# Norm factors moved behind the products in the second block, and a mirrored Fourier stage

## The chip, the cores and the metric

The kernel runs as one program on one core of a Trainium2 chip. The metric is the device time of one execution in microseconds (us); the median of several executions is compared. A profiled execution is recorded once for each kernel, and all rows below come from it.

## The reference

Two blocks follow each other on one sequence of 512 positions with 1024 channels, all in float32. The first block also carries 256 context positions and has a Fourier layer and a recurrent layer, each followed by a mixture of experts. The second has two layers with a mixer (gated MLP, state-space part, latent attention) and a squared-ReLU MLP. What matters here:

```python
def rmsnorm_2(x, g):
    var = jnp.mean(xf * xf, axis=-1, keepdims=True)
    return (xf * lax.rsqrt(var + EPS)).astype(x.dtype) * g

def fourier_mix(h, w_o, b_o):           # 4 groups of 256 channels, positions and channels transformed
    f = jnp.fft.fft2(hg, axes=(1, 3), norm='ortho').real
    return f.reshape(bsz, t, D_MODEL).astype(h.dtype) @ w_o + b_o

x = rmsnorm(x, final_g)                 # end of the first block
for l in range(DEPTH):                  # second block, DEPTH = 2
    h = rmsnorm_2(x, norm_mix_g[l])
    uv, z, xbc, dt_raw, c_q, c_kv, k_rope = split_cols(h @ w_in[l])
    ...                                 # latent attention: rmsnorm_2(c_q, ..) @ w_qb, rmsnorm_2(c_kv, ..) @ w_kvb
    x = x + mix @ w_out[l]
    x = x + squared_relu_mlp(rmsnorm_2(x, norm_mlp_g[l]), mlp_w1[l], mlp_w2[l])
return rmsnorm_2(x, final_norm_g)
```

Since the MLP squares its ReLU, a positive factor on its input comes out as its square on its output.

## The kernel before

Channels lie on the 128 partitions in eight tiles (`KT`), positions along the free axis: `X` holds the residual stream, `H` the normalised input of a stage, `scr` is a scratch area that stages carve up by offset (`S(off, ...)`). Weights stream through a ring of eight slots of 1 MB in the fixed order of `weight_plan`; SyncE issues the load of a slot as soon as the slot's last reader is done. PSUM has eight banks that `bank()` hands out in turn; the next user waits for `free.<name>`. Each engine has one counting semaphore; `did` counts and names steps, `later`/`at` wait for a named step. Each engine runs the list of stages in its own order; `phase()` at the end of a stage makes an engine wait until the other engines have ended that stage too, except, for TensorE, VectorE and ScalarE, in `mla` and `mix`.

A float32 matmul appears in the profile as two records; the MLP's are of another kind, one record each: its operands are split into a rounded high part and the rest (`HHI`, `WHI` on ScalarE, the rests on VectorE), and three products are made of them (L2571 to L2573, L2586 to L2588).

A norm (`fg`, `n20`, `n30`, `n21`, `n31`, `end`) is squares on ScalarE (L371 or L387), their sum over tiles on VectorE (L379), a product with ones on TensorE (L418), the reciprocal root on ScalarE (L393), and eight multiplies of `X` with gain and factor into `H` on VectorE (L434). Squares and sums of most tiles are made as the residual tiles come (`residual_scalar`, `residual_vector`, L538/L540). After `moe1` come `fg`, a copy of H to X (L2783), and `n20`. Then `mla` makes six latent products (L1961 three of c_q, L1970 two of c_kv, L1976 rotary key with dt), the sums of their squares (L1984), the products q (L1992, six), k (L2002) and v (L2007), and scores (L2021). VectorE turns the rotary parts (L2110 to L2116 for k, L2129 to L2134 for q) and applies the latent norms (L2124). `wout` makes the output products (L2313), `mlp` follows.

The Fourier stage makes for each of 6 position tiles and 4 channel groups a product with cosine and sine of 256 (512 columns, L561), evicted to `Z`; then for each of 8 channel tiles and both segments the products with the position tables (L574), evicted to `H` (L601); then the output products (L520). Between them stand blocks of the adaLN parameters (`ada_tensor`, L454 and L463), 1 MB of weights each.

Of the kernel before, what the change touches and what calls it, by code (L numbers as in the profile page):

```python
# [25 lines left out]
P = 128  # L26
# [109 lines left out]
def build(nc, a, out, table):  # L136
# [3 lines left out]
    with ctx:  # L140
# [143 lines left out]
        DFT_C = S(12288, 2, 512)  # L284
# [77 lines left out]
        NEXT = {"moe0": "n1", "post": "m1", "moe1": "fg", "wout0": "n30", "mlp0": "n21", "wout1": "n31", "mlp1": "end"}  # L362
        EARLY = list(NEXT.values()) if STOP is None else list(NEXT.values())[:-1]

        def residual_scalar(act, tag, segs, norm, tiles=range(KT)):

            w = sum(s[1] for s in segs)
            for m in tiles if norm in EARLY else ():
                if later(act, f"{tag}.x{m}"):
                    act.wait_ge(*at(f"{tag}.x{m}"))  # L370
                did(A_, act.activation(H[:, m, 0:w], X[:, m, 0:w], ACT.Square).then_inc(scalar_done, 1), f"{norm}.sq{m}")  # L371

        def norm_sum(dve, norm, k, w):
# [3 lines left out]
            if later(dve, f"{norm}.sq0"):  # L377
                dve.wait_ge(*at(f"{norm}.sq0"))
            did(V, dve.tensor_tensor(H[:, 0, 0:w], H[:, 0, 0:w], H[:, k, 0:w], ALU.add).then_inc(vector_done, 1))  # L379
# [32 lines left out]

        def norm_tensor(pe, tag, segs):
# [24 lines left out]
        small_rs = S(SCRW - TA, TA)  # L438

# [88 lines left out]
        def residual_vector(dve, tag, segs, gate=None, norm=None, tiles=range(KT)):  # L528
# [4 lines left out]
            for m in tiles:  # L533
                for i, (s0, sn) in enumerate(segs):
                    t = tile(dve, f"{tag}.{m}.{s0}")
                    x = X[:, m, s0:s0 + sn]
                    if gate is None:
# [4 lines left out]
                marks[f"{tag}.x{m}"] = (V, count[V])  # L542
                if norm in EARLY and m >= 2:
                    norm_sum(dve, norm, m - 1, w)
            if norm in EARLY and KT - 1 in tiles:
# [3 lines left out]
        Z = S(0, 6, 4, 512)  # L549
        fb = small[:, 0:16].rearrange("p (k c) -> p k c", c=2)  # L550

        def fnet_tensor(pe):
            if later(pe, "dft"):
                pe.wait_ge(*at("dft"))
            for tt in range(6):
                for g in range(4):
                    b = bank(pe, f"f1.{tt}.{g}")
                    for k in range(2):
                        if later(pe, f"n0.h{2 * g + k}"):
                            pe.wait_ge(*at(f"n0.h{2 * g + k}"))  # L560
                        ins = pe.matmul(b, H[:, 2 * g + k, tt * P:tt * P + P], DFT_C[:, k, :], start=k == 0, stop=k == 1)  # L561
                    did(T_, ins.then_inc(tensor_done, 1), f"f1.{tt}.{g}")
                    if (4 * tt + g) % 3 == 2:
                        ada_tensor(pe, ADA_F1[0] + (4 * tt + g) // 3)
            for s0, sn, tts in ((TX, TC, (4, 5)), (0, TX, (0, 1, 2, 3))):
                for d in range(KT):
                    b = bank(pe, f"f2.{d}.{s0}")
                    for cs in range(2):
                        for n, tt in enumerate(tts):
                            if later(pe, f"free.f1.{tt}.{d // 2}"):  # L570
                                pe.wait_ge(*at(f"free.f1.{tt}.{d // 2}"))
                            rhs = DFT_T[:, n, cs * TX:cs * TX + TX] if s0 == 0 else DFT_TC[:, n, cs * TC:cs * TC + TC]
                            o = cs * 256 + (d % 2) * P
                            ins = pe.matmul(b[:, 0:sn], Z[:, tt, d // 2, o:o + P], rhs,  # L574
                                            start=cs == 0 and n == 0, stop=cs == 1 and n == len(tts) - 1)
                    did(T_, ins.then_inc(tensor_done, 1), f"f2.{d}.{s0}")
                    if d % 2:
                        ada_tensor(pe, ADA_F2[0] + (0 if s0 else 4) + d // 2)
            linear_tensor(pe, "fo", "fwo", lambda k, s0, sn: H[:, k, s0:s0 + sn], SEGS, lambda k: f"free.f2.{k}.0",
                          between=lambda n: ada_tensor(pe, ADA_FO[0] + n))  # L580

        def fnet_scalar(act):
            for tt in range(6):
# [2424 lines left out]
```

## Time and profile before

| | |
|---|---|
| median of 3 runs | 4090.1 us (4081.94 to 4090.91) |
| profiled execution, its own time | 4094.43 us |
| its span, first to last instruction | 4092.6 us |
| TensorE busy | 3697.3 us, 90% of the span |
| VectorE busy | 1310.9 us, 32% |
| ScalarE busy | 1017.0 us, 25% |
| mean granted TensorE clock | 0.959 |

A busy time says how long an engine had work, not whether that work held anything up; for that the chain of work that ended last is read, and the timeline of the stretch. The granted clock is a share of 2.4 GHz and is either 1.00 or 0.50, so a mean between them is a stretch that holds both. Spacing from one start to the next is used for the length of a product, because the recorded ends of pipelined matmuls overlap.

### The profile page before, as it was taken

What the parts mean: (1) busy time and instruction counts of PE and PEld (TensorE: products, weight loads), DVE (VectorE), ACT (ScalarE), POOL (GpSimd) and SP (SyncE); (2) the same over time, 40 slices, a digit from 0 to 9 for tenths busy, and PEclk for the clock granted to TensorE, in tenths of its full rate; (3) what the DMA queues carried; (4) which work ended last, traced back from release to release, by engine and by line L of the source; (5) the groups of instructions that cost most, each with busy time, mean ns of one, the idle gap of its engine ahead of it and who ended that gap; (6) DMA issues with size and microseconds to landing.
All of it is one profiled execution on the core that took longest, in us unless ns stands there. A gap on an engine that the chain in (4) does not pass through costs nothing.

```text
span 4092.6 us, 63317 instructions
## 1 busy us (share of the span) xinstructions
PE 3697.3 (90%) x28370; PEld 2279.9 (56%) x28370; DVE 1310.9 (32%) x2368; ACT 1017.0 (25%) x1974; POOL 260.6 (6%) x232
## 2 busy tenths in 40 slices
PE   6998999999799989998867887879989998998998
PEld 3556443433357678888352332235548884656886
DVE  2123000000443167776330000025433333444342
ACT  3012011111143155454110000114322221423231
POOL 0000000000000144433000000000000000000000
PEclk9987999999889999999979999989999999999999
DMA  8345889898035244332429999901222322112320
GB/s 292 103 139 173 306 307 362 313 351 294 0 141 183 65 112 92 68 83 77 141 103 381 375 375 387 351 23 48 71 62 93 93 83 77 48 52 78 98 97 21
DMA packets 530928, 666.74 MB, mean 163 GB/s; under 512 B 156553, under 2 KB 299145, under 8 KB 530657
## 3 DMA queue, kind: packets, MB, share of 16 engines
q1 hardware_dynamic: 520544, 633.40, 45.8%
q10 hardware_dynamic: 6912, 18.88, 1.2%
q0 software_dynamic: 3200, 10.42, 0.7%
q8 instruction: 223, 3.65, 0.4%
q14 instruction: 49, 0.39, 0.0%
HBM read 631.18 MB, written 31.46 MB: 162 GB/s over the span
## 4 chain that ended last, share of the span: by engine, by line
PE 76%; DVE 8%; DMA 5%; SPq 4%; ACT 3%; POOL 3%; issue 1%; DVEq 0%; ACTq 0%; POOLq 0%
PE ps L657 12%; PE ps L662 4%; DMA ring<-in_moe_wu 4%; SPq L2710 4%; PE ps L520 3%; PE ps L850 3%; PE ps L2571 3%; PE ps L2572 3%; PE ps L2573 3%; PE ps L2587 3%; PE ps L2588 3%; PE ps L2586 3%; PE ps L823 3%; PE ps L2207 3%; PE ps L2313 3%; POOL ring L1403 3%
## 5 line engine op out<-in xcount | busy, mean ns | idle before, releaser
L657 PE MATMUL ps<-ring,H 128*64 128x512 f32 x2048 | 494.2, 601 | 52.1 <-DMA ring<-in_moe_wu 39.2
L657 PEld LDWEIGHTS ps<-ring,H 128*64 128x64 f32 x2048 | 147.3, 137 | 343.0 <-issue 252.4
L759 DVE TENSOR_TENSOR scr<-ps,scr 128x512 f32<-128x512 f32 x32 | 22.1, 692 | 965.5 <-PE ps L662 516.9
L657 PE MATMUL ps<-ring,scr 128*64 128x512 f32 x1024 | 248.3, 599 | 40.3 <-DMA ring<-in_moe_wd 38.8
L2571 PE MATMUL ps<-scr_rounded,ring_rounded 128*128 128x512 f32 x512 | 204.8, 400 | 23.0 <-ACT scr_rounded L2609 23.0
L2640 DVE TENSOR_TENSOR ring_rounded<-ring,scr_rounded 128x2048 fp32r<-128x2048 f32 x64 | 146.7, 2293 | 227.6 <-ACT scr_rounded L2606 227.5
L2572 PE MATMUL ps<-H_rounded,scr_rounded 128*128 128x512 f32 x512 | 204.6, 400 | 0.0
L2573 PE MATMUL ps<-scr_rounded 128*128 128x512 f32 x512 | 204.3, 399 | 0.0
L2588 PE MATMUL ps<-scr_rounded 128*128 128x512 f32 x512 | 202.5, 395 | 0.0
L2586 PE MATMUL ps<-scr_rounded,ring_rounded 128*128 128x512 f32 x512 | 201.8, 394 | 0.0
L2606 ACT ACTIVATE scr_rounded<-ring 128x2048 fp32r<-128x2048 f32 x64 | 122.1, 1907 | 257.7 <-PE ps L2588 246.4
L657 PEld LDWEIGHTS ps<-ring,scr 128*64 128x64 f32 x1024 | 72.9, 136 | 189.2 <-issue 125.1
L850 PE MATMUL ps<-scr 128*128 128x512 f32 (+1 forms) x320 | 125.9, 556 | 4.2 <-ACT scr L733 2.9
L823 PE MATMUL ps<-scr 128*128 128x256 f32 x512 | 121.4, 390 | 4.0 <-DVE scr L930 4.0
L2571 PEld LDWEIGHTS ps<-scr_rounded,ring_rounded 128*128 128x128 f32 x512 | 97.5, 190 | 48.8 <-DVE H_rounded L2645 24.6
L662 PE MATMUL ps<-ring,H 128*32 128x256 f32 x2048 | 123.8, 382 | 0.0
L727 ACT ACTIVATE scr<-ps 64x512 f32<-64x512 f32 x64 | 37.9, 592 | 313.0 <-PE ps L662 161.5
L2207 PE MATMUL ps<-H,ring 128*128 128x512 f32 x256 | 111.3, 594 | 0.0
L2572 PEld LDWEIGHTS ps<-H_rounded,scr_rounded 128*128 128x128 f32 x512 | 97.6, 191 | 23.6
L2313 PE MATMUL ps<-scr,ring 128*128 128x512 f32 x256 | 110.7, 593 | 0.0
L2573 PEld LDWEIGHTS ps<-scr_rounded 128*128 128x128 f32 x512 | 97.3, 190 | 23.6
L2586 PEld LDWEIGHTS ps<-scr_rounded,ring_rounded 128*128 128x128 f32 x512 | 96.1, 188 | 23.9
(403 smaller groups left out, 6123.9 us busy)
## 6 DMA issues: line engine op xcount, KB each, us to landing
ring<-in_moe_wg SPq DMA_DIRECT2D x128, 1024.0 KB, 9.5
ring<-in_moe_wu SPq DMA_DIRECT2D x128, 1024.0 KB, 8.6
ring<-in_moe_wd SPq DMA_DIRECT2D x128, 1024.0 KB, 10.3
ring<-in_mlp_w SPq DMA_DIRECT2D x64, 1024.0 KB, 5.5
ring<-in_ada_w SPq DMA_DIRECT2D x48, 1024.0 KB, 7.4
ring<-in_w_in SPq DMA_DIRECT2D x14, 1024.0 KB, 5.2
ring<-in_w_out SPq DMA_DIRECT2D x8, 1024.0 KB, 5.1
st_kka<-scr ACTq DMA_DIRECT2D x16, 384.0 KB, 3.5
```

What stands on the lines that cost most here:

```text
L657: ins = pe.matmul(bx[64 * n:64 * n + 64, :], stat_x(k), w[:, k % 4, :], start=k == 0, stop=k == KT - 1)
L662: ins = pe.matmul(bc[32 * n:32 * n + 32, 0:256], stat_c(k), w[:, k % 4, o:o + 256], start=k == 0, stop=k == KT - 1)
L823: ins = pe.matmul(b[:, 0:256], HT[:, tt, k * P:k * P + P], GM[:, tt, :], start=tt == 0, stop=tt == 3)
L850: ins = pe.matmul(b[:, 0:sn], ys[:, j, m * P:m * P + P], sm[:, j, :], start=j == 0, stop=j == nj - 1)
L2207: ins = pe.matmul(b, w[:, k, (m % 2) * P:(m % 2) * P + P], H[:, k, 0:TX], start=k == 0, stop=k == KT - 1)
L2313: ins = pe.matmul(banks[m], w[:, k, (m % 2) * P:(m % 2) * P + P], MIX[:, k, :], start=k == 5, stop=k == 4)
L2571: pe.matmul(b, low[:, k, o], hh, start=k == 0, stop=False)
L2572: pe.matmul(b, high[:, k, o], hl, start=False, stop=False)
L2573: ins = pe.matmul(b, high[:, k, o], hh, start=False, stop=k == KT - 1)
L2586: pe.matmul(banks[m], low[:, k, o], hh, start=f == 0, stop=False)
L2588: ins = pe.matmul(banks[m], high[:, k, o], hh, start=False, stop=f == 15)
L2710: did(f"slot{i % NSLOT}", sp.dma_start(dst, src.rearrange("(k p) c -> p k c", p=min(P, rows))).then_inc(sems[f"slot{i % NSLOT}"], 16), "w. ...
```

## The change

Second block: the stages between `moe1` and the end lose `fg`, and no engine waits for the others at the end of `moe1`, `n2*`, `n3*`, `wout*`, `mlp*` (GpSimd still does). `residual_vector` writes the unnormalised `H = gain * X` per tile, and ScalarE squares X elsewhere (`SQUARES`), for `n20` also gain times X. `fg` and `n20` become one pass: with q0 and q1 the two mean squares, the factor for `n20` is the reciprocal root of q1 + eps*(q0 + eps), and X itself is scaled later. The latent products take the unnormalised H; the sum product runs behind the first of them; the latent norms need no factor (only eps is scaled by the mean square), the rotary key and dt are multiplied by it, then all of H. For `n3*`, high and low parts of H are made tile by tile during `wout`, the sum product runs behind the first MLP product, and `1/(mean square + eps)` multiplies each second MLP product before it is added. The last norm keeps its form; its result leaves in four stores.

Fourier: the channel transform of a group makes 129 cosine and 127 sine columns (256 in place of 512). Cosine column 128 of the four groups is gathered in `ZH` and transformed once per segment. The second transform makes four blocks per segment; the mirrored channels are the same block read backwards in position, and `fnet_wo`'s rows are permuted to fit.

```diff
-            if e != "G" and name[:3] in ("mla", "mix"):
+            if e != "G" and (name[:3] in ("mla", "mix", "wou", "mlp") or name[:2] in ("n2", "n3") or name == "moe1"):
...
+            if norm in SQUARES:
+                for m in tiles:
+                    if later(act, f"{tag}.x{m}"):
+                        act.wait_ge(*at(f"{tag}.x{m}"))
+                    for n, sq in enumerate(SQUARES[norm]):
+                        scale = col("final_g", m) if n else 1.0
+                        did(A_, act.activation(sq[:, m, :], X[:, m, 0:TX], ACT.Square, scale=scale).then_inc(scalar_done, 1))
...
+        def scaled_vector(dve, norm, m):
+            dve.wait_ge(*own(dve, V))
+            l = int(norm[2])
+            if norm == "n20":
+                ins = dve.tensor_scalar(H[:, m, 0:TX], X[:, m, 0:TX], col("final_g", m), col("nmix", m), ALU.mult, ALU.mult)
+            else:
+                ins = dve.tensor_scalar(H[:, m, 0:TX], X[:, m, 0:TX], col("nmix" if norm == "n21" else "nmlp", 8 * l + m), None, ALU.mult)
+            did(V, ins.then_inc(vector_done, 1), f"{norm}.u{m}")
+
+        def low_vector(dve, norm, m):
+            t0 = HIGH[norm]
+            if later(dve, f"{t0}hh{m}"):
+                dve.wait_ge(*at(f"{t0}hh{m}"))
+            did(V, dve.tensor_tensor(H_r[:, m, 0:TX], H[:, m, 0:TX], HHI[:, m, :].bitcast(F32), ALU.subtract).then_inc(vector_done, 1), f"{t0}hl{m}")
...
+                    if scale is not None:
+                        dve.wait_ge(*own(dve, V))
+                        did(V, dve.tensor_tensor(scale[1], t, scale[0], ALU.mult).then_inc(vector_done, 1), f"free.{tag}.{m}.{s0}")
+                        dve.wait_ge(*own(dve, V))
+                        did(V, dve.tensor_tensor(x, scale[1], x, ALU.add).then_inc(vector_done, 1))
+                        continue
...
+                if norm in SQUARES:
+                    scaled_vector(dve, norm, m)
+                    if norm in HIGH and m == 6:
+                        low_weights(dve, int(norm[2]), 0)
+                    if norm in HIGH and m:
+                        low_vector(dve, norm, m - 1)
...
             for tt in range(6):
+                for gg in range(2):
+                    b = bank(pe, f"f1.{tt}.{gg}")
+                    for g in (2 * gg, 2 * gg + 1):
+                        o = 256 * (g % 2)
+                        for k in range(2):
+                            ins = pe.matmul(b[:, o:o + 256], H[:, 2 * g + k, tt * P:tt * P + P], DFT_C[:, k, :], start=k == 0, stop=k == 1)
+                    did(T_, ins.then_inc(tensor_done, 1), f"f1.{tt}.{gg}")
+                    if (2 * tt + gg) % 3 < 2:
+                        ada_tensor(pe, ADA_F1[0] + (2 * tt + gg) // 3 * 2 + (2 * tt + gg) % 3)
...
+                for g in (0, 2):
+                    t = tile(dve, f"f2.{g}.{s0}")
+                    did(V, dve.tensor_copy(H[:, 2 * g + 1, s0 + 1:s0 + sn], t[:, sn - 1:0:-1]).then_inc(vector_done, 1))
+                    did(V, dve.tensor_copy(H[:, 2 * g + 1, s0:s0 + 1], t[:, 0:1]).then_inc(vector_done, 1))
+                    did(V, dve.tensor_copy(H[:, 2 * g, s0:s0 + sn], t[:, 0:sn]).then_inc(vector_done, 1), f"free.f2.{g}.{s0}")
...
+            latent("cq", 0, f"{t0}cq.0", 0)
+            sums_tensor(pe, hk)
+            latent("cq", 1, f"{t0}cq.0", P)
+            latent("cq", 2, f"{t0}cq.1", 0)
+            latent("ckv", 0, f"{t0}ckv", 0)
+            latent_norm("cq", 3)
+            latent("ckv", 1, f"{t0}ckv", P)
+            latent("kr", "", f"{t0}kr", 0)
+            latent_norm("ckv", 2)
...
+            for k in range(KT):
+                did(V, dve.tensor_tensor(H[:, k, 0:TX], H[:, k, 0:TX], RMS, ALU.mult).then_inc(vector_done, 1), f"{hk}.h{k}")
+            for k in range(KT) if l == 0 else ():
+                did(V, dve.scalar_tensor_tensor(X[:, k, 0:TX], X[:, k, 0:TX], col("final_g", k), RMS1, ALU.mult, ALU.mult).then_inc(vector_done, 1))
             for h in range(6):
...
+                        if f == 0:
+                            sums_tensor(pe, f"n3{l}")
...
+            low_weights(dve, l, 1)
+            mean_vector(dve, f"n3{l}", MSQ)
+            did(V, dve.reciprocal(MSQ, MSQ).then_inc(vector_done, 1))
...
+            for k in range(0, KT, 2):
+                if later(sp, f"end.h{k + 1}"):
+                    sp.wait_ge(*at(f"end.h{k + 1}"))
+                did("out", sp.dma_start(out.rearrange("(k p) t -> p k t", p=P)[:, k:k + 2], H[:, k:k + 2, 0:TX]).then_inc(output_out, 16), by=16)
```

## Rows read from the trace of the kernel before

**Rows 1.** The page, part 4: shares of the chain that ended last.

```profile
PE 76%; DVE 8%; DMA 5%; SPq 4%; ACT 3%; POOL 3%; issue 1%; DVEq 0%; ACTq 0%; POOLq 0%
```

**Rows 2.** TensorE's timeline, Fourier stage: start, us, line, operation, shape, count, idle before.

```profile
61.49 5.42 PE L561 MATMUL ps<-scr,H 128*128 128x512 f32 x12
66.84 1.07 PE L454 MATMUL ps<-ring,csil 128*32 128x256 f32 x16
114.18 3.70 PE L574 MATMUL ps<-scr 128*128 128x256 f32 x16
117.81 1.07 PE L454 MATMUL ps<-ring,csil 128*32 128x256 f32 x16
119.28 3.70 PE L574 MATMUL ps<-scr 128*128 128x256 f32 x16
129.47 13.98 PE L574 MATMUL ps<-scr 128*128 128x512 f32 x32
144.85 13.98 PE L574 MATMUL ps<-scr 128*128 128x512 f32 x32
```

**Rows 3.** TensorE's timeline from moe1 to layer 0's first score.

```profile
2689.76 7.03 PE L850 MATMUL ps<-scr 128*128 128x512 f32 x16
2725.58 22.67 PE L1961 MATMUL ps<-H,ring 128*128 128x512 f32 x48 [6.26 <-DVE H L434]
...
2803.48 0.39 PE L2021 MATMUL ps<-scr 96*128 96x128 f32 x2
```

**Rows 4.** Timeline of VectorE there: the multiplies of the second norm.

```profile
2720.14 5.39 DVE L434 SCALAR_TENSOR_TENSOR H<-X,vec,scr 128x512 f32<-128x512 f32 x8 [3.00 <-ACT scr L393]
```

**Rows 5.** Timeline of TensorE: mlp0's last product and layer 1's first score.

```profile
3395.14 0.40 PE L2588 MATMUL ps<-scr_rounded 128*128 128x512 f32 x1
...
3483.30 0.39 PE L2021 MATMUL ps<-scr 96*128 96x128 f32 x2
```

**Rows 6.** Timelines: layer 0's last residual add (VectorE), first MLP product (TensorE).

```profile
3018.98 0.69 DVE L538 TENSOR_TENSOR X<-ps,X 128x512 f32<-128x512 f32 x1 [5.58 <-PE ps L2313]
...
3033.82 0.77 PE L2571 MATMUL ps<-scr_rounded,ring_rounded 128*128 128x512 f32 x1 [11.51 <-ACT scr_rounded L2609]
```

**Rows 7.** The page, part 5: busy us, mean ns, idle before, releaser.

```profile
L2571 PE MATMUL ps<-scr_rounded,ring_rounded 128*128 128x512 f32 x512 | 204.8, 400 | 23.0 <-ACT scr_rounded L2609 23.0
L2640 DVE TENSOR_TENSOR ring_rounded<-ring,scr_rounded 128x2048 fp32r<-128x2048 f32 x64 | 146.7, 2293 | 227.6 <-ACT scr_rounded L2606 227.5
```

**Rows 8.** The output: SyncE's timeline, and the DMA issues (KB, us to landing).

```profile
4084.99 0.38 SPq L2717 DMA_DIRECT2D outT<-H  x1
...
outT<-H SPq DMA_DIRECT2D x1, 2048.0 KB, 7.2
```

**Rows 9.** Windows: us; busy by engine; granted clock; DMA share; GB/s.

```profile
54.00:58.00 4.00, 4.00 (x7) 1.73 (x8) 0.69 (x1) 0.00 (x0) 0.00 (x0) 0.67 1.10 348
78.00:82.00 4.00, 4.00 (x27) 1.75 (x26) 0.69 (x1) 0.98 (x2) 0.00 (x0) 1.00 0.32 110
300.00:312.00 12.00, 12.00 (x92) 6.26 (x84) 11.96 (x16) 3.19 (x12) 0.00 (x0) 0.50 0.88 281
3038.00:3040.00 2.00, 2.00 (x6) 1.54 (x6) 2.00 (x1) 0.00 (x0) 0.00 (x0) 0.53 0.00 0
```

**Rows 10.** VectorE's timeline in layer 0's latent attention, before the scores.

```profile
2768.99 0.68 DVE L2110 COPY scr<-ps 6x512 f32<-6x512 f32 x1 [43.46 <-PE ps L1976]
2773.72 3.60 DVE L2124 SCALAR_TENSOR_TENSOR scr<-scr,vec 128x512 f32<-128x512 f32 x5
2780.38 0.69 DVE L2129 TENSOR_TENSOR scr<-ps,scr 32x512 f32<-32x512 f32 x1 [3.06 <-PE ps L1992]
```

**Rows 11.** The chain that ended last: start, us, what, records.

```profile
2761.99 6.88 PE ps L1976 x16
2775.95 17.39 PE ps L1992 x36
...
4069.77 0.23 PE ps L2586
```

More of the change, by code:

```diff
@@ L411, in norm_scalar, with sums_tensor, mean_vector @@
                 shift_scalar(act, tag, segs)
+        def scaled_vector(dve, norm, m):
[11 more added lines that the diff above has]
+            did(V, dve.tensor_tensor(H_r[:, m, 0:TX], H[:, m, 0:TX], HHI[:, m, :].bitcast(F32), ALU.subtract).then_inc(vector_done, 1), f"{t0}hl{m}")
+        def sums_tensor(pe, norm):
+            if later(pe, f"{norm}.sum"):
+                pe.wait_ge(*at(f"{norm}.sum"))
+            for n, sq in enumerate(SQUARES[norm]):
+                b = bank(pe, f"{norm}.ss{n}")
+                did(T_, pe.matmul(b, ones[:, :], sq[:, 0, :], start=True, stop=True).then_inc(tensor_done, 1), f"{norm}.ss{n}")
+        def mean_vector(dve, norm, to, tmp=None):
+            t = tile(dve, f"{norm}.ss0")
+            if norm == "n20":
+                did(V, dve.tensor_scalar(tmp, t, 1.0 / D, EPS, ALU.mult, ALU.add).then_inc(vector_done, 1), f"free.{norm}.ss0")
+                t = tile(dve, f"{norm}.ss1")
+                did(V, dve.tensor_scalar(to, t, 1.0 / D, None, ALU.mult).then_inc(vector_done, 1), f"free.{norm}.ss1")
+                dve.wait_ge(*own(dve, V))
+                did(V, dve.scalar_tensor_tensor(to, tmp, EPS, to, ALU.mult, ALU.add).then_inc(vector_done, 1))
+            else:
+                did(V, dve.tensor_scalar(to, t, 1.0 / D, EPS, ALU.mult, ALU.add).then_inc(vector_done, 1), f"free.{norm}.ss0")
+            marks[f"{norm}.mean"] = (V, count[V])
+            dve.wait_ge(*own(dve, V))
         def norm_tensor(pe, tag, segs):
@@ L555, in fnet_tensor @@
             for tt in range(6):
-                for g in range(4):
[L557 to L564, printed above, removed]
@@ new lines, in fnet_tensor, with table_of @@
+            for s0, sn, tts in ((TX, TC, (4, 5)), (0, TX, (0, 1, 2, 3))):
+                def table_of(n, cs):
+                    return DFT_T[:, n, cs * TX:cs * TX + TX] if s0 == 0 else DFT_TC[:, n, cs * TC:cs * TC + TC]
+                for tt in tts:
+                    for gg in range(2):
+                        if later(pe, f"free.f1.{tt}.{gg}"):
+                            pe.wait_ge(*at(f"free.f1.{tt}.{gg}"))
+                b = bank(pe, f"fh.{s0}")
+                for n, tt in enumerate(tts):
+                    ins = pe.matmul(b[:, 0:sn], ZH[:, tt, :], table_of(n, 0), start=n == 0, stop=n == len(tts) - 1)
+                did(T_, ins.then_inc(tensor_done, 1), f"fh.{s0}")
+                for g in range(4):
+                    b = bank(pe, f"f2.{g}.{s0}")
@@ L568, in fnet_tensor @@
                     for cs in range(2):
                         for n, tt in enumerate(tts):
[L570 to L574, printed above, removed]
+                            ins = pe.matmul(b[:, 0:sn], Z[:, tt, g, cs * P:cs * P + P], table_of(n, cs),
@@ L1918, in build @@
         MIX = S(0, KT, TX)
+        MEAN, RMS, MEAN1, RMS1 = (MIX[:, n, :] for n in range(4))
         CQ = S(4096, 3, TX)
@@ L2850, in _ @@
                     norm_scalar(act, st, XSEG, True)
[L2851 removed]
+                elif st == "end":
                     norm_scalar(act, st, XSEG, False)
```

265 lines of the change are left out of this document (157 added, 108 removed).

## The prediction

> **What bounds the kernel now.** I read the page first. TensorE holds 76% of the chain that ended last, VectorE 8%, ScalarE 3% [rows 1]. So time can be won in two ways: fewer TensorE columns where TensorE never waits, or closing the holes in which it waits for a chain of short instructions on the other two. Then I read the timeline of TensorE at the two places that the diff touches.
>
> The Fourier stage has no holes. In the first transform twelve records of 512 columns and one adaLN block alternate; in the second the period is 5.10 us (114.18 to 119.28) for the 256 context positions and 15.38 us for the 512 positions, each with one adaLN block of 1.47 us (117.81 to 119.28) [rows 2].
>
> In the second block there are holes. The last product of moe1 ends at 2696.8 (2689.76 + 7.03), mla0's first starts at 2725.58: 28.8 us, two norms one behind the other [rows 3], each a sum product, a root on ScalarE and eight multiplies of 5.39 us on VectorE [rows 4]. A shorter one follows mlp0, whose last product ends about 3395.4 [rows 5]. Layer 0's output products end just before VectorE's add at 3018.98, at about 3018.9; the MLP starts at 3033.82, 14.95 us later [rows 6]. Both layers have this hole: the group of the first MLP products shows 23.0 us of idle in all behind ScalarE's high parts, 11.5 per layer [rows 7]. At the end one store goes out at 4084.99 and lands 7.2 us later [rows 8]. After each hole TensorE also runs at 1.2 GHz for a while: after 3033.82 the granted clock is 0.50 until nearly 3040 (0.53 over the last 2 us) [rows 9].
>
> **Fourier stage, first transform.** 12 groups of 4 products of 256 columns take the place of 24 groups of 2 products of 512. It stays at 96 records. A 512-column record takes 5.35/12 = 0.446 us (61.49 to 66.84), one of 256 columns 3.63/16 = 0.227 [rows 2]: 42.8 becomes 21.8, 21.0 less. Two things are given back. The last group now has no adaLN block behind it, so the second transform waits for its eviction, two copies and a one-column copy: between nothing and three operations of 0.7 [rows 10]; I take 1.3, as the copies are 256 wide. And the warm-up: the stage starts at 1.2 GHz, and the clock rises after some 3 us of dense products (mean 0.67 over 54 to 58) [rows 9]. Now 3.4 us of products are followed by a light adaLN block, and such blocks alone left the clock at 0.50 for the 12 us from 300 to 312 [rows 9]. Bounds: nothing if it rises in the first group, 7.5 us if it takes the two groups that stand back to back (18 us at half speed cost 9, of which 1.5 is paid today). I take 2. Gain 21.0 - 1.3 - 2 = 17.7 us.
>
> Could the adaLN weights be late? They come at 348 GB/s with the queues full (share 1.10); over 78 to 82 the share is 0.32, so by then the eight-deep ring was full and waited for TensorE [rows 9]. ada.15, the last that the stage needs, was therefore in before 78; the shorter stage wants it at about 83. No wait.
>
> **Second transform.** One half-spectrum block and four blocks per segment in place of eight. Context: 4 x 5.10 = 20.4 becomes 4 x (8 x 0.227 + 1.47) + 4 x 0.227 = 14.1. The 512 positions, a record (15.38 - 1.47)/32 = 0.435: 61.5 becomes 4 x (16 x 0.435 + 1.47) + 8 x 0.435 = 37.2 [rows 2]. 30.6 us less. The mirrored evictions (reverse copy, copy, one column, one row) are in no row; four operations of 0.7 make 2.8 us, under 8.4 us per group, and the last group has an adaLN block and six products, 1.5 + 5.2 us, ahead of its first reader. Cost nothing; 2 us if reverse reads took three times as long. Fourier together 48.3 us.
>
> **moe1 to the first score of layer 0.** The unnormalised h is written while moe1's last products run (eight products, 6.9 us per tile; VectorE needs 2.6), so mla0's first product starts at once and only its eighth matmul waits for the last tile. From there: six latent products of 6.88 = 41.3, five latent sums 4.3, q 36 x 0.430 = 15.5 [rows 11], k and v 2803.48 - 2775.95 - 17.39 = 10.1 [rows 3, 11]: 71.2 us, and 0.86 for each norm's sum product (two records). Layer 0 has two: 72.9. Today it is 2803.48 - 2696.8 = 106.7 [rows 3].
> What is late next is VectorE. It sits at the latent sum until 47.2 us; k's rope, broadcast and the latent norms today take 2768.99 to 2777.3, 8.3 us, of which three of five norms, 2.2, come earlier now [rows 10]; two new operations of 0.7 come on top, then H times the factor and X times gain and factor, 5.4 each by the nearest row [rows 4]. The q ropes start near 47.2 + 6.1 + 1.4 + 10.8 = 65.5, each three operations, 2.1 us [rows 10]. k's third product needs the bank of q0, and so on to the first score, which needs that of q5: 65.5 + 5 x 2.1 + 1.4 = 77.4. So 4.5 us of delay; bounds 0 (small waits overlap) and 8. Gain 106.7 - 77.4 = 29.3. It holds two spells of half clock: 22.67 us for 48 records that take 20.6, and 17.39 for 36 that take 15.5 [rows 3, 11].
>
> **mlp0 to the first score of layer 1.** Today 3483.30 - 3395.4 = 87.9 [rows 5]. Afterwards 71.2 + 0.9 = 72.1; X gets no second norm, the ropes start near 60 and q5's bank is free at 72. Gain 15.8, bounds 13 and 16.
>
> **Output products to MLP, twice.** Per tile VectorE adds, scales, subtracts the high part and sums, four operations of 0.5 to 0.7, 2.6 us against tiles of 2.6 and then 6.9 us; the weight split, 2.3 us [rows 7], goes behind tile 6 under 6.9 us. The last low tile comes 3.4 us behind the last product; the first MLP product wants it after 21 matmuls of 0.234 [rows 11], 4.9 us. No hole: 14.95 us, and 3.0 for 6.1 us at half clock [rows 6, 9], less 0.86 for the sum product: 17.1, twice 34.2. Bounds 15 and 18 each.
> Behind the products stand a reciprocal (no row; even 5 us, once per layer) and one more multiply per residual tile. They lie in weight slots of 48 x 0.234 = 11.2 us, of which VectorE has 2.3 + 4 x 0.7 = 5.1 in use [rows 7, 10, 11]. Without that cover 16 tiles per layer would cost 22 us in all.
>
> **End.** One more multiply, +0.7. The output leaves in four stores, the first 4.0 us before the last multiply ends. If bytes bound it, the end is 4081 + 7.2 = 4088.2 in place of 4092.2 [rows 8]; if nothing of the store shrinks but its start, 2 us less is won. 3.3, bounds 1 and 4.
>
> **Sum.** 48.3 + 29.3 + 15.8 + 34.2 + 3.3 = 130.9. The profiled execution took 4094.4 (span 4092.6 and 1.8 around it); 3963.5. The median shown is 4.3 below the profiled run: 3959.2; for small waits that I left out I say 3961.
>
> **Rivals.** (a) The first transform stays at 1.2 GHz: 96 x 0.454 + 8 x 2.6 (12 us hold 92 records, 20 per block [rows 9]) = 64 us in place of 37, time 3988. For it: adaLN blocks never raised the clock. Against it: two groups stand back to back in every third place, 6.8 us, longer than the 3 to 6 us after which it rose at 57 and 3040 [rows 9]. Chance 0.05. The Trainium skill (TensorE: Matmul & The Clock Gate, "What's actually happening") says that the throttled state is the default and that activity releases it; by that rule the thinned first transform could be kept slow, the 27 us above, where I take 2; the row at 300 agrees with it, the row at 54 does not decide [rows 9].
> (b) VectorE is late behind the norms by more than summed: 4 us more in each latent stage, 3 us in front of each MLP, reverse reads 2: 3977. For it: its work in these stretches doubles. Chance 0.08.
> (c) Slower than before: VectorE sets the MLP's pace. All 64 slots would have to grow by 131/64 = 2.0 us, so VectorE would need 13.3 us per slot where it uses 5.1, price 64 us per microsecond beyond. Time over 4100. The split's row has more idle (227.6) than work (146.7) [rows 7]. Chance 0.01.
> (d) The holes close but the clock does not stay up, 9 us back, and the stores win nothing: 3973. Chance 0.08.
> Forecast, 3945 to 3970: 0.78.
>
> **Numbers.** 0.2%, about what a measurement can tell, is 8 us; all cases but (c) lie far beyond. The range takes the lower bounds and the runs' own spread (9 us) below, (b) and (d) and the other bounds above, and leaves out (a) and (c): 3942 to 3985. Faster 0.98, same 0.01, slower 0.01.
>
> **What would show it.** The second transform starts near 91, the stage's output products near 142; mla0's first product stands directly behind moe1's last; no TensorE hole over 1 us before either MLP and clock 1.00 there; the k to score stretch is stretched by 4.5 us in layer 0 and hardly in layer 1. The prediction is wrong if TensorE waits for VectorE over 8 us before a first score, or if adaLN blocks near 75 still run at half clock.

## The result, and the profile after

The changed kernel took 3956.6 us (median of 4 runs, 3954.8 to 3959.3) beside 4086.5 us for the kernel before on the same chip (4 runs, 4081.9 to 4090.9): a ratio of 0.9683, with a 95% interval of 0.9666 to 0.970. The forecast was 3961.0, the range 3942 to 3985. The profiled execution took 3957.2 us; its span is 3955.4 where the kernel before had 4092.6, so 137.2 us went.

First the page of the changed kernel: part 4 (shares of the chain that ended last) and two rows of part 5 (busy us, mean ns, idle before).

```profile
PE 76%; DVE 9%; DMA 5%; SPq 4%; ACT 3%; POOL 2%; issue 1%; DVEq 0%; ACTq 0%; POOLq 0%
...
L2725 DVE TENSOR_TENSOR ring_rounded<-ring,scr_rounded 128x2048 fp32r<-128x2048 f32 x64 | 146.7, 2292 | 218.9 <-ACT scr_rounded L2718 218.6
L2743 PE MATMUL ps<-scr_rounded,ring_rounded 128*128 128x512 f32 x512 | 203.6, 398 | 0.0
```

The shares hardly moved, since the whole shrank by only 3%. The second of the two groups is the one with 23.0 us of idle in [rows 7]: now it has none.

TensorE's timeline of the Fourier stage in the changed kernel (start, us, line, shape, count, idle before and who ended it), and windows with the granted clock behind the POOL column:

```profile
54.26 3.59 PE L645 MATMUL ps<-scr,H 128*128 128x256 f32 x8 [10.51 <-ACT H L427]
57.78 1.07 PE L519 MATMUL ps<-ring,csil 128*32 128x256 f32 x16
58.78 1.99 PE L645 MATMUL ps<-scr,H 128*128 128x256 f32 x8
...
87.58 1.97 PE L645 MATMUL ps<-scr,H 128*128 128x256 f32 x8
90.46 1.10 PE L658 MATMUL ps<-scr 128*128 128x256 f32 x4 [0.91 <-ACT scr L680]
...
116.75 7.11 PE L664 MATMUL ps<-scr 128*128 128x512 f32 x16
...
142.28 4.11 PE L585 MATMUL ps<-H,ring 128*128 128x512 f32 x9
```

```profile
54.00:58.00 4.00, 3.74 (x12) 2.66 (x16) 0.82 (x3) 0.16 (x1) 0.00 (x0) 0.55 1.10 348
58.00:62.00 4.00, 4.00 (x43) 2.41 (x35) 0.78 (x3) 1.26 (x5) 0.00 (x0) 1.00 1.10 349
```

The first group of eight products runs at 1.2 GHz (3.59 us), the second at 2.4 (1.99 us). The adaLN block between them does not bring the clock down (1.00 from 58 to 62). Where the two transforms meet, TensorE waits 0.91 us for the last eviction.

TensorE from moe1's last product to the first scores of layer 0, then VectorE in the same stretch, then TensorE in front of layer 1's first score, all of the changed kernel:

```profile
2643.75 2.74 PE L972 MATMUL ps<-scr 128*128 128x512 f32 x6
2646.32 7.03 PE L2084 MATMUL ps<-H,ring 128*128 128x512 f32 x16
...
2719.08 1.56 PE L2125 MATMUL ps<-ring,scr 128*128 128x384 f32 x4 [0.60 <-DVE scr L2283]
2721.24 1.56 PE L2125 MATMUL ps<-ring,scr 128*128 128x384 f32 x4 [0.60 <-DVE scr L2283]
2723.49 0.46 PE L2139 MATMUL ps<-scr 96*128 96x128 f32 x2 [0.70 <-DVE scr L2283]
```

```profile
2700.88 4.91 DVE L2275 TENSOR_TENSOR H<-H,scr 128x512 f32<-128x512 f32 x8
2705.71 5.39 DVE L2277 SCALAR_TENSOR_TENSOR X<-X,vec,scr 128x512 f32<-128x512 f32 x8
2711.12 0.69 DVE L2280 TENSOR_TENSOR scr<-ps,scr 32x512 f32<-32x512 f32 x1
```

```profile
3363.20 5.32 PE L2125 MATMUL ps<-ring,scr 128*128 128x384 f32 x16
3368.36 0.39 PE L2139 MATMUL ps<-scr 96*128 96x128 f32 x2
```

The 28.8 us between the first two lines of [rows 3] are gone: mla0's first product stands directly behind moe1's last. What is late next is VectorE: its query rotations (L2280 to L2285) begin at 2711.12, behind the eight multiplies of H and the eight of X, and TensorE waits for them in front of each group of four value products and at the score: 0.18, three times 0.60 and 0.70 us of idle. In layer 1, where X gets no factor, the score waits for nothing.

At the MLP (TensorE in layer 0), and at the end (SyncE and the DMA issues of the end: KB, us to landing):

```profile
2924.57 12.61 PE L2466 MATMUL ps<-scr,ring 128*128 128x512 f32 x29
2936.61 0.79 PE L2743 MATMUL ps<-scr_rounded,ring_rounded 128*128 128x512 f32 x1
```

```profile
3946.33 5.39 DVE L495 SCALAR_TENSOR_TENSOR H<-X,vec,scr 128x512 f32<-128x512 f32 x8 [2.16 <-ACT scr L417]
3947.77 4.35 SPq L2873 DMA_DIRECT2D outT<-H  x4
```

```profile
outT<-H SPq DMA_DIRECT2D x4, 512.0 KB, 3.3
```

The first MLP product follows the output products without a wait, where [rows 6] had 11.51 us of idle. The granted clock from 2936 to 2944 is 1.00.

### The profile page after: what moved, and what is told of

Its sections match the earlier page's. It is cut to its first block, busy times and chain, and to the rows that moved or that the text cites. A ratio compares the mean times of both kernels' runs of the same rounds, so it can differ in the third digit from the quotient of the medians.

```text
span 3955.4 us, 63217 instructions
## 1 busy us (share of the span) xinstructions
PE 3628.6 (92%) x28286; PEld 2254.3 (57%) x28286; DVE 1341.8 (34%) x2430; ACT 1018.0 (26%) x1996; POOL 260.2 (7%) x232
## 4 chain that ended last, share of the span: by engine, by line
PE 76%; DVE 9%; DMA 5%; SPq 4%; ACT 3%; POOL 2%; issue 1%; DVEq 0%; ACTq 0%; POOLq 0%
PE ps L779 12%; PE ps L784 5%; DMA ring<-in_moe_wu 4%; SPq L2865 4%; PE ps L585 3%; PE ps L972 3%; PE ps L2745 3%; PE ps L2761 3%; PE ps L2762 3%; PE ps L2744 3%; PE ps L2760 3%; PE ps L2743 3%; PE ps L945 3%; PE ps L2360 3%; PE ps L2466 3%; PE ps L2084 2%
## 5 line engine op out<-in xcount | busy, mean ns | idle before, releaser
L972 PE MATMUL ps<-scr 128*128 128x512 f32 (+1 forms) x320 | 125.9, 556 | 4.2 <-ACT scr L855 2.9
L611 DVE SCALAR_TENSOR_TENSOR X<-ps,ada,X 128x512 f32<-128x512 f32 (+1 forms) x48 | 31.8, 662 | 241.8 <-PE ps L972 119.9
L862 ACT ACTIVATE scr<-ps 128x512 f32<-128x512 f32 x32 | 19.1, 597 | 358.7 <-PE ps L784 196.2
L2743 PEld LDWEIGHTS ps<-scr_rounded,ring_rounded 128*128 128x128 f32 x512 | 96.1, 188 | 24.3 <-issue 1.0
## 6 DMA issues: line engine op xcount, KB each, us to landing
ring<-in_ada_w SPq DMA_DIRECT2D x48, 1024.0 KB, 10.3
```

The costliest lines, as they stand in the source:

```text
L972: ins = pe.matmul(b[:, 0:sn], ys[:, j, m * P:m * P + P], sm[:, j, :], start=j == 0, stop=j == nj - 1)
L2743: pe.matmul(b, low[:, k, o], hh, start=k == 0, stop=False)
```

## The experiments

All twelve profiled executions beside the two kernels, cut at starts of TensorE products (the last cut at the span's end). Times are us of the traces; the names of the columns say what a stretch ends with (for a score, the product with the identity that starts 0.2 to 0.3 us behind it): the Fourier stage's first product, the first output product of that stage, the first router product of moe0, the last product of moe0, that of moe1, the first score of layer 0, the first product of mlp0, the first score of layer 1, the end.

```
                      start Fourier router  moe0    moe1  score0  mlp0  score1   end
before                 53.8  137.2  131.8  758.9  1614.5  107.5  230.1  449.7  609.1
changed                54.3   88.0  125.9  759.5  1618.2   77.9  212.8  432.0  586.8
e1 Fourier alone       53.8   88.0  125.9  759.5  1614.8  107.5  230.1  449.7  609.7
e2 block 2 alone       52.4  138.5  125.7  759.2  1615.0   77.9  212.9  431.9  587.1
e3 engines meet        52.4   87.8  125.9  759.4  1615.2   83.9  217.3  439.5  595.8
e6 scale twice         53.3   88.7  131.2  758.8  1614.5   77.9  212.8  432.0  588.7
e7 changed again       53.1   88.6  131.2  758.8  1611.3   77.9  212.9  431.9  587.2
e4 one store           53.5   88.1  126.0  759.5  1618.0   77.9  212.8  431.9  593.5
e5 X's norm later      54.8   88.3  126.0  756.5  1611.8   73.6  212.8  432.0  586.2
e8 interleaved         53.3   88.7  117.3  758.9  1614.6   78.0  212.8  432.0  587.0
e9 both                54.9   88.6  117.3  758.9  1613.6   73.6  214.6  431.9  586.9
e11 interleaved again  54.2   89.1  117.4  759.2  1617.2   77.9  214.6  431.9  587.7
e10 before, interl.    52.8  138.6  119.0  759.2  1614.6  107.5  230.1  449.7  609.8
e12 before, no meet.   54.8  137.7  125.3  759.0  1611.3  101.7  228.4  443.4  609.0
```

Read the table by columns. Where an edit does not touch a stretch, most stretches repeat within a microsecond. The exceptions are the router column, which has two values for one kernel (below), the moe1 column (1611.3 to 1618.2, in no relation to any edit; what varies there, no run shows), moe0 in e5 (756.5), the Fourier column (up to 1.4 us apart) and the column that ends with mlp0 (212.8 or 214.6). That last difference lies in the mixer, where the granted clock stands at 0.50 for 6.8 us (2822.4 to 2829.2 in the changed kernel) or for 10.3 (2899.9 to 2910.2 in the kernel before).

### e1 and e2: each part alone

e1 is the kernel before with the new Fourier stage:

```diff
-        DFT_C = S(12288, 2, 512)
+        DFT_C = S(12288, 2, 256)
...
-    c["dftC"] = np.concatenate([cs, sn], 1)
+    c["dftC"] = np.concatenate([cs[:, 0:129], sn[:, 1:128]], 1)
...
+    n["fnet_wo"] = n["fnet_wo"][:, np.concatenate([mirrored[:, 0:128], mirrored[:, 128:256]], 1).reshape(-1), :]
...
```

with the new `fnet_tensor`, `fnet_scalar` and copies of `fnet_vector`; e2 is the changed kernel with those lines and functions put back.

> The kernel before with the mirrored Fourier stage and nothing else of the change. Theory of the prediction: the two parts add, so 4086.5 less 17.7 for the first transform and 30.6 for the second, 48.3 in all, gives 4038 us (ratio 0.988), with the first transform at 36 to 38 us of the trace, the second at 51 to 53 and the output projection unchanged. Rival: the first transform runs at half the clock here and wins nothing, 4056 us. Rival: the shorter stage meets weights that come no earlier and waits for them behind the stage, 4050 us or more. The second block must take what it took in the kernel before.

> The changed kernel with the old Fourier stage, its table and the old order of the output weights. Theory of the prediction: 29.3 + 15.8 + 34.2 + 3.3 = 82.6 us less than 4086.5, so 4004 us (ratio 0.980). In the trace of the changed kernel 5.9 us of the gain were in the norm in front of the first mixture of experts, where the instructions are the same and only TensorE's granted clock differs: if that is a matter of chance, this run's stage takes either 36 or 42 us, whatever the Fourier stage is. Rival: that difference comes from the Fourier stage, so this run has 42 us there and the run with the Fourier stage alone has 36.

e1 took 4039.0 us and e2 4005.5 (4038 and 4004 were expected), beside 4089.4 for the kernel before in that set: ratios 0.9868 (0.9852 to 0.9885) and 0.9791 (0.9776 to 0.9806). Their product is 0.966, the whole change 0.968 (0.9666 to 0.970): within these intervals the parts add. In the table e1 changes the Fourier column by 49.2 us and no column of the second block, and e2 the reverse. The router column is 125.9 and 125.7 in both, so these runs give its 5.9 us to neither part; e7, below, shows them come and go in one program.

### e3 and e12: the meetings of the engines

e3 is the changed kernel with the old rule, e12 the kernel before with most of the new one:

```diff
 # e3
-            if e != "G" and (name[:3] in ("mla", "mix", "wou", "mlp") or name[:2] in ("n2", "n3") or name == "moe1"):
+            if e != "G" and name[:3] in ("mla", "mix"):
 # e12
-            if e != "G" and name[:3] in ("mla", "mix"):
+            if e != "G" and (name[:3] in ("mla", "mix", "wou") or name[:2] == "n2" or name == "moe1"):
```

> The changed kernel, but all engines meet again at the end of each stage of the second block, apart from the attention and mixer stages, as in the kernel before. The factors stay behind the products. Theory A (the gain comes from the products that need no finished norm; the meetings are a smaller part): TensorE then waits at four places (behind the last expert product, behind both output projections and behind the first MLP) for one eviction of 0.7 us, one scaling of 0.7 us, one square and one sum, 3.5 to 4.5 us each, and 1 us each for the clock: 16 to 22 us more than the changed kernel, 3973 to 3979 us. Theory B (the meetings were what cost the time): 60 us or more come back, 4017 us or more. Theory C (meetings are free where the next products wait for the same data): within 4 us of the changed kernel.

> The kernel before without the meeting of the engines behind the last experts, behind both output projections and behind the norm in front of each attention stage (the two norms in front of the MLPs, the final norm of the first block and the MLPs still end in one). Theory A (a meeting costs only where the next products have their data): the products still wait for the finished norm; what is won is that the first of them follows the first norm tile and not the eighth, 1.5 to 2 us at each of two places: 4082 to 4084 us, within 0.15 per cent of the kernel before. Theory B (the meetings cost by themselves what they cost in the changed kernel): at least 12 of its 23 us, 4074 us or less.

e3 took 3980.9 us (ratio 0.9733, 0.9716 to 0.9749), 23 to 24 more than the changed kernel: theory A, a little over the upper end of its 16 to 22. TensorE in e3 behind moe1 and in front of mlp0:

```profile
2645.31 8.83 PE L2084 MATMUL ps<-H,ring 128*128 128x512 f32 x16 [4.02 <-DVE scr L398]
...
2941.85 0.50 PE L2743 MATMUL ps<-scr_rounded,ring_rounded 128*128 128x512 f32 x1 [3.90 <-DVE scr L398]
```

The waits are 4.02 and 3.90 us (3.4 behind mlp0), as expected. The clock's part was too small in the expectation: the 16 latent products take 8.83 us, where they take 7.03 in the changed kernel. With its clock a meeting costs 5.6 to 6.3 us: 6.0 behind moe1, 6.3 behind mlp0, and 4.5 in front of each MLP with 1.2 more in the MLP's first 48 products, which the next column holds. In the last column 3.3 of the 9.0 us come from light mixer products of layer 1 that happened to run at 1.2 GHz.

e12 took 4072.9 us (ratio 0.9971, 0.996 to 0.9983), 13.4 less than the kernel before. By the number that is theory B (at least 12 us), not A's 2 to 4; by the mechanism most of it is what A names, the earlier start, which brings more than A gave it. The table has 13.8 us in three columns, 5.8, 1.7 and 6.3. VectorE's multiplies of the second norm and TensorE's first products in e12:

```profile
2711.99 5.39 DVE L434 SCALAR_TENSOR_TENSOR H<-X,vec,scr 128x512 f32<-128x512 f32 x8 [3.00 <-ACT scr L393]
2712.88 23.21 PE L1961 MATMUL ps<-H,ring 128*128 128x512 f32 x48 [1.71 <-DVE H L434]
```

Here the products start 0.9 us behind the first multiply; in the kernel before it was 5.44 ([rows 3], [rows 4]). I had reckoned with products at 2.4 GHz, which would have caught up with the multiplies and then gone at their pace, so that only the last tile counted. But TensorE comes out of a long wait at 1.2 GHz. The 48 products take 23.21 us in e12 and 22.67 in the kernel before: at that clock they are no faster than the multiplies, so of a start 4.5 us earlier 4.0 are kept, and the low clock lies beside VectorE's work. The other 1.7 of the first column's 5.8 are the query products, which here take 15.69 us and not the 17.39 of [rows 11]: the wait that they stand behind is the same 2.80 us in both, but the clock did not fall. In the third column the start is again 4.5 us earlier, of which 4.4 are kept; 0.6 are the norm's sum product and 1.3 the first products of mlp0, both less at 1.2 GHz, as is the middle column's 1.7, the mixer. So 8.4 of the 13.8 us are the earlier starts. The other 5.3 are shorter spells of 1.2 GHz; whether they follow from the edit or fell that way by chance, no run shows. So of the second block's 83 us (the sum of its terms) some 13, 8 of them traced to the earlier starts, could be had without moving a factor, about 59 without touching the meetings (83 less the 24 of e3), and the last 11 only with both.

### e6: is VectorE's room in the MLP real?

```diff
                     if scale is not None:
                         dve.wait_ge(*own(dve, V))
+                        did(V, dve.tensor_tensor(scale[1], t, scale[0], ALU.mult).then_inc(vector_done, 1))
+                        dve.wait_ge(*own(dve, V))
                         did(V, dve.tensor_tensor(scale[1], t, scale[0], ALU.mult).then_inc(vector_done, 1), f"free.{tag}.{m}.{s0}")
```

> The changed kernel with the multiplication of an MLP product by the reciprocal mean square done twice for each of the 16 tiles of each MLP: 32 more VectorE instructions of 0.69 us, 22 us of VectorE. Theory of the prediction: VectorE has room under the products in all but the last group of four tiles of each MLP, where up to 4 x 0.69 = 2.8 us lie open, so 1.4 to 5.5 us more than the changed kernel, 3958 to 3962 us. Rival (VectorE sets the pace of the MLP): all 22 us come back, 3979 us or more.

e6 took 3953.7 us (ratio 0.9667, 0.9652 to 0.9681): no loss that can be measured, of 22 us of added work. The score1 column does not move (432.0), the last one grows by 1.5 to 1.9 us, which is all that shows of the 1.4 to 5.5 expected. The prediction's cover holds, and rival (c) is out.

### e4: the four stores

```diff
-            for k in range(0, KT, 2):
-                if later(sp, f"end.h{k + 1}"):
-                    sp.wait_ge(*at(f"end.h{k + 1}"))
-                did("out", sp.dma_start(out.rearrange("(k p) t -> p k t", p=P)[:, k:k + 2], H[:, k:k + 2, 0:TX]).then_inc(output_out, 16), by=16)
+            if later(sp, f"end.h{KT - 1}"):
+                sp.wait_ge(*at(f"end.h{KT - 1}"))
+            did("out", sp.dma_start(out.rearrange("(k p) t -> p k t", p=P), H[:, :, 0:TX]).then_inc(output_out, 16), by=16)
```

> The changed kernel once more, as the measure for the three others of this set: 3956.6 us if nothing changes. The norm in front of the first mixture of experts (first square to first router product) takes 36 or 42 us of the trace: 36 again speaks for a difference that belongs to the kernel, 42 for chance.

> The changed kernel with the output stored by one transfer behind the last tile instead of four. Prediction: the single 2048 KB store took 7.2 us to land, a quarter of it 3.3 us, so 3.3 to 3.9 us more than the changed kernel, 3960 us. Rival (the stores win nothing, the end was shorter for another reason): no difference.

e7, the changed kernel again, took 3957.7 us and e4 3964.2, 6.4 more, where 3.3 to 3.9 were expected. VectorE's last multiplies and SyncE's store in e4, and the landing:

```profile
3948.07 5.39 DVE L495 SCALAR_TENSOR_TENSOR H<-X,vec,scr 128x512 f32<-128x512 f32 x8 [3.11 <-ACT scr L417]
3953.49 0.38 SPq L2872 DMA_DIRECT2D outT<-H  x1
```

```profile
outT<-H SPq DMA_DIRECT2D x1, 2048.0 KB, 7.3
```

From the last multiply's end to the span's end it is 3961.2 - 3953.46 = 7.7 us in e4, and 3955.4 - 3951.72 = 3.7 in the changed kernel: the stores are worth 4.0 us. The rest of the 6.7 us by which the last column of this execution grows is the clock's and not the store's: about 1.0 at the norm's sum product (2.08 us in place of 1.13), and 1.6 in the mixer of layer 1. Where the other executions lost the 2.4 us beyond the store's 4.0, no trace shows.

### e5: what is late next

```diff
-            for k in range(KT) if l == 0 else ():
-                did(V, dve.scalar_tensor_tensor(X[:, k, 0:TX], X[:, k, 0:TX], col("final_g", k), RMS1, ALU.mult, ALU.mult).then_inc(vector_done, 1))
             for h in range(6):
                 t = tile(dve, f"{t0}q{h}")
...
             did(V, dve.tensor_tensor_scan(DT4, RS6, DT0, 0.0, ALU.mult, ALU.add).then_inc(vector_done, 1), f"{t0}ac")
+            for k in range(KT) if l == 0 else ():
+                did(V, dve.scalar_tensor_tensor(X[:, k, 0:TX], X[:, k, 0:TX], col("final_g", k), RMS1, ALU.mult, ALU.mult).then_inc(vector_done, 1))
```

> The changed kernel, but the eight VectorE instructions of 0.67 us that put the final norm of the first block into the residual (5.3 us) stand no longer in front of the query rotations but in the mixer, in front of the convolution. Theory of the prediction: VectorE arrives last at the first scores of layer 0, so TensorE's 4.3 us of waits there go, and the mixer has VectorE idle for 13 us at the new place: 4 to 5 us less, 3952 us. Rival: the first score waits for the key or value evictions of ScalarE as well, so only 1 us is won. Rival: the mixer's convolution is then late, nothing is won.

TensorE in e5 in front of the first score:

```profile
2705.64 5.33 PE L2125 MATMUL ps<-ring,scr 128*128 128x384 f32 x16
2710.80 0.39 PE L2139 MATMUL ps<-scr 96*128 96x128 f32 x2
```

All 16 value products run in one piece and nothing is waited for. The score0 column goes from 77.9 to 73.6, by the 4.3 us expected, and the mixer's column stays at 212.8. In the times it shows less: 3956.4 us beside 3957.7, with single runs from 3943.8 to 3963.2. The 3943.8 is the execution of the trace, which was also 3.0 us shorter in moe0 and 6.4 in moe1 than the changed kernel's, where the edit has no part. The two intervals (0.9672 to 0.9699 and 0.967 to 0.9697) do not tell 4 us from none.

### e8, e10, e11 and e9: the clock in front of moe0

The instructions there are the same in both kernels, yet the changed one was 5.9 us faster. Windows of the changed kernel, then of e7, the same program once more (granted clock behind the POOL column):

```profile
238.00:250.00 12.00, 11.60 (x68) 6.55 (x68) 2.66 (x3) 3.97 (x17) 0.00 (x0) 0.52 0.98 299
250.00:258.00 8.00, 8.00 (x94) 4.34 (x96) 6.75 (x6) 4.11 (x14) 0.00 (x0) 0.87 0.75 241
```

```profile
238.00:250.00 12.00, 12.00 (x76) 6.35 (x80) 2.09 (x3) 4.33 (x15) 0.00 (x0) 0.53 1.02 313
250.00:258.00 8.00, 8.00 (x60) 4.36 (x56) 7.91 (x8) 2.11 (x8) 0.00 (x0) 0.50 0.77 249
```

One program, two courses: in both executions the clock falls at 238, but in the one it is back by 252, in the other it stays down over all blocks of the condition's product. The router column is 126 in one and 131 in the other. Of the ten executions without the edit below, seven had 125.3 to 126.0 and three 131.2 to 131.8. The Trainium skill (TensorE: Matmul & The Clock Gate, "What's actually happening") says that the point at which the clock rises differs from run to run of one kernel; the two pairs of lines agree. The difference that the Trainium skill gives there is half a microsecond; here the clock is back at 252 in one execution and at 297 in the other.

What makes it fall is in TensorE's timeline of the changed kernel: 3.68 us of idle behind ScalarE, which takes eight squares in one go before it evicts a block.

```profile
233.65 1.07 PE L519 MATMUL ps<-ring,csil 128*32 128x256 f32 x16
238.40 0.98 PE L528 MATMUL ps<-vec,scr 128*128 128x2 f32 x4 [3.68 <-ACT scr L544]
239.31 1.93 PE L519 MATMUL ps<-ring,csil 128*32 128x256 f32 x16
```

e8 puts an eviction behind every second square (e11 is e8 again, e10 the same edit in the kernel before, e9 both e5 and e8):

```diff
-                    squares_scalar(act, st, SEGS)
-                    for b in range(ADA_M0[0], half):
+                    for k in range(KT):
+                        did(A_, act.activation(H[:, k, 0:TA], X[:, k, 0:TA], ACT.Square).then_inc(scalar_done, 1), f"{st}.sq{k}")
+                        if k % 2:
+                            ada_scalar(act, ADA_M0[0] + k // 2)
+                    for b in range(ADA_M0[0] + 4, half):
                         ada_scalar(act, b)
```

> The changed kernel, but in the norm in front of the first mixture of experts ScalarE takes two squares, then the eviction of one block of the condition's product, and so on, where it took all eight squares first. In the trace TensorE stood for 3.68 us behind those squares, and its granted clock fell from 1.0 to about 0.5 behind it. Theory: without the stand TensorE keeps the clock, the sum product comes at 243 us of the trace in place of 247.6 and the stage ends 4 to 5 us earlier, 3952 us; if the clock fell for longer in the kernel before, the same edit would win 10 us there. Rival: the clock falls for the small products themselves, not for the stand, and only 1 to 2 us are won.

> The kernel with the interleaved squares once more, as the measure for the one before it in this set: 3946 us, with the stretch to the router at 117.3 us again, since TensorE does not stand there long enough for the chance of two outcomes that the changed kernel has (125.9 or 131.2).

> The kernel before with the interleaved squares only. Its stretch from the output projection's first product to the router took 131.8 us in its profiled execution. Theory (the stand behind the squares lowers the clock, and how long it stays low is chance): 117 us here too, so 8.6 to 14.5 us less than the kernel before, 4072 to 4078 us. Rival (the Fourier stage's change decides how long the clock is low): the edit wins 14 us in every execution.

> The changed kernel with both edits: the residual's final norm moved into the mixer, and the squares of the norm in front of the first mixture of experts taken in turn with the evictions of the condition's blocks. In the traces the first took 4.3 us off the stretch from the last expert product to the first score (77.9 to 73.6), the second brought the stretch from the output projection's first product to the router to 117.3 us from 125.9 or 131.2. The stretches are far apart, so they add: 3946.2 - 4.3 = 3942 us. Rival, from the times of the first edit alone (3956.4 beside 3957.7): it is given back where the trace did not look, and this kernel stays at 3945 to 3947 us.

e8 took 3946.2 us and e11 3946.5: 10 to 11.5 less than the changed kernel, about twice what was expected. The window of e8:

```profile
238.00:250.00 12.00, 11.12 (x128) 6.58 (x127) 9.44 (x9) 7.36 (x24) 0.00 (x0) 1.00 1.12 337
```

The clock stays at 1.00 and the router column is 117.3 and 117.4. The expectation took a sum product 4.6 us earlier; it came 6.8 us earlier (240.85 in place of 247.67), and the blocks behind it, which the expectation forgot, also run at 2.4 GHz now.

e10 took 4081.3 us beside 4086.2 (ratio 0.999, 0.9981 to 0.9999): 5 us, less than the 8.6 to 14.5 expected. Its interval reaches to 7.8 us, and 125.3 (the column in e12) less 119.0 is 6.3, so it fits if the kernel before mostly has the shorter course; how often it has, no run shows. e10's clock was not held throughout, though TensorE never stood there for more than 0.6 us at a time:

```profile
290.50:293.90 3.40, 3.40 (x16) 1.26 (x19) 0.18 (x1) 1.16 (x2) 0.00 (x0) 0.50 1.15 309
```

Its two sum products of the norm took 2.78 us, in e8 1.56. So without the stand the clock was held in three executions of four; the rival, that it falls for the small products themselves, is not quite out, though in e10 it cost 1.7 us (119.0 beside 117.3) and not 8.6 to 13.9.

e9 took 3944.6 us (ratio 0.9657, 0.9644 to 0.967), the lowest median of all. Both columns moved as expected, but beside e11 it is 1.9 us less and not 4.3; again the spread of single runs (3940.8 to 3951.1 in e11) hides that much.

## Why the prediction was right, step by step

```
term                                   predicted   trace of the change
first transform                          -17.7     -19.1  (55.3 -> 36.2)
second transform                         -30.6     -30.1  (81.9 -> 51.8)
moe1's end to layer 0's first score      -29.3     -29.5  (106.7 -> 77.2)
mlp0's end to layer 1's first score      -15.8     -15.8  (87.9 -> 72.1)
output products to MLP, twice            -34.2     -34.3  (17.4 and 16.9)
end                                       -3.3      -3.7  (17.9 -> 14.2)
sum                                     -130.9    -132.5
```

- **First transform.** The last eviction was waited for 0.91 us where I took 1.3. The warm-up, priced at 2 us over that of today, cost hardly any over it: the first eight products took 3.59 us in place of 1.99, 1.6 in all, and in the kernel before the first twelve had already paid 1.4 (6.80 us in place of 5.40). About 0.5 of this was given back, since a group of eight takes 1.91 us from start to start and not 8 x 0.227. Rival (a), 27 us more at 1.2 GHz, did not occur in any of the runs with the new stage (Fourier column 87.8 to 89.1). By the rule that the prediction cites from the Trainium skill (TensorE: Matmul & The Clock Gate, "What's actually happening"), that activity releases the throttle, the thinned stage could have stayed slow; the trace shows that it did not, with a granted clock of 1.00 from 58 us to the end of the stage. The rival's ground that adaLN blocks never raised the clock holds only for the rows it was read from: in the changed kernel the clock rises at 252 among such blocks, though only behind the norm's sum product.
- **Second transform.** Eight products take 1.89 to 1.97 us and sixteen 7.03 to 7.11 as reckoned. The mirrored evictions, which no row showed, stayed hidden. The 0.5 us too much are the same groups of eight and the 0.1 that a group of sixteen takes over 16 x 0.435.
- **moe1 to the first score.** Both halves of the step hold: no hole behind moe1, and VectorE late by 4.3 us (4.5 forecast), which e5 takes away. The rotations began 64.8 us behind moe1's end, 65.5 forecast. Rival (b), VectorE later still, did not occur.
- **mlp0 to the next first score.** By the sum, with no wait of VectorE.
- **Output products to MLP.** No hole and no low clock. e3 shows what holds it together: a single wait of 3.4 to 4.0 us costs 5.6 to 6.3.
- **MLP's cover.** The reciprocal takes 3.35 us (5 allowed) and no MLP is longer for the further multiplies; e6 doubles them, and that costs 1.5 to 1.9 us at the end of the last MLP and nothing elsewhere.
- **End.** The stores bring 4.0 us, the added multiply takes a part back.

Of the 137.2 us that the span lost, 132.5 are in these terms. Another 5.9 are the router stretch and 3.5 both mixers, and the other stretches took 4.7 more. The first comes and goes in one program, as e7 shows. The mixers' 3.5 are two shorter spells of 1.2 GHz (6.8 us where the kernel before, e1 and e10 have 10.3 each time); e4, e9 and e11 have the longer spell in one mixer each, e12 the shorter one in one, so it is in part chance, and how far the change itself shortens it, no run shows. Of the 4.7, 3.7 are moe1, within what that column varies by.

That the forecast of 3961.0 came within 4.4 us is partly luck. The profiled execution took 3957.2 us and 3963.5 had been summed for it, 6.3 less: 1.6 in the terms, and 4.7 where gains and losses that the prediction did not know of (9.4 and 4.7) meet. The median was then put 4.3 us below the profiled execution, as in the kernel before, where it lies 0.6 below, and 1.8 us were put on for small waits: 6.3 - 3.7 + 1.8 = 4.4.

What the prediction did not separate is that the second block's gain holds two edits that in part need each other: the factors behind the products (some 59 us without the rest) and the dropped meetings (13 alone, 24 on top of the factors).

## What to carry to other kernels

In this kernel a wait of 3.4 to 4.0 us on TensorE cost half as much again or more with the slower products behind it (5.6 to 6.3 in all), so the last small waits are worth attention too; and products that started 4.5 us early at 1.2 GHz beside another engine's chain kept 4.0 us of it. A factor that is the same for a column can wait behind the products; then ask which engine has to apply it, in front of whom it stands in that engine's queue, and whether it can go behind work that is awaited. When two traces differ where the programs do not, run the same program twice before explaining it.

## What the runs showed of the hardware

- One program had two courses of the clock behind one stand of 3.68 us: back at 2.4 GHz after some 14 us, or not for the rest of that stage, 5.3 us apart (125.9 and 131.2). Without the stand the stretch took 117.3 or 117.4 in e8, e9 and e11, and 119.0 in e10, where the clock fell all the same, for 3.4 us.
- Evictions that read a PSUM tile backwards cost hardly more than forward ones, 558 ns in the mean beside 548. VectorE's groups of the changed kernel in the second transform (busy, mean ns of one):

```profile
L715 DVE COPY H<-ps 128x255 f32<-128x255 f32 (+1 forms) x4 | 2.2, 558 | 41.2 <-PE ps L664 41.2
L717 DVE COPY H<-ps 128x256 f32<-128x256 f32 (+1 forms) x4 | 2.2, 548 | 0.0
```

- Four stores of 512 KB issued while the tiles are finished end 3.7 us behind the last multiply (changed kernel); one of 2048 KB ends 7.7 us behind it (e4).
